# A fourth buffer of probabilities and three tiles of row maxima and exponents ahead, in the attention of the third layer

## The chip, the cores and the metric

The kernel is one program on one NeuronCore of a Trainium2 chip. Its metric is the device time of a whole call in microseconds (us), as the median of several executions; lower is better. A core has five engines that run their own instruction streams in program order and meet only at semaphores: TensorE (PE in the profile), VectorE (DVE), ScalarE (ACT), GpSimd (POOL) and SyncE (SP, which starts the loads).

## The reference, cut to what matters

Three layers work on 256 latent tokens and 256 context tokens of width 1024. The first mixes an mLSTM with window attention, the second mixes retention with a state space scan, the third is a multi-head latent attention; each is followed by a feed-forward part. In all of them the latent tokens end up as the output. What the change touches is the core of the third layer's attention:

```
q: 16 heads x 256 latent queries x 96        (64 plain + 32 rotated)
k: 16 heads x 512 keys (context + latent) x 96
v: 16 heads x 512 keys x 64
for each head:  p = softmax(q k^T / sqrt(96));  o = p v      # 256 x 512, then 256 x 64
out = concat(o) @ w_out
```

## The kernel before, in words

The attention works on 32 tiles, `a` = 0 to 31. A tile is one head with one half (128) of the queries against all 512 keys. Four successive tiles hold both halves of two heads (`head_of`), so the tiles go in groups of four. Each engine has its own loop over the tiles, written out by hand, and the order within an engine is fixed by it. Five steps make a tile, in this chain:

- **scores(a)**, PE, line 873: one product of 96 x 128 by 96 x 512 into one of four PSUM banks (0, 1, 6, 7 by `a % 4`); for a >= 4 it waits until the exponents of tile a - 4 have been taken from that bank. In the profile it is two MATMUL records a tile, under the names `bank` (tiles 0 and 1 of a group) and `cond_a` (tiles 2 and 3).
- **peaks(a)**, DVE, lines 2099 and 2100: the row maximum of the scores, and its product with the negative scale of the query. It waits for scores(a).
- **exps(a)**, ACT, line 1248: exponents of the scores into the buffer `prob[a % 3]`, with their row sum. It waits for peaks(a), and for the transposes of tile a - 3, which read the same buffer.
- **divide(a)**, DVE, lines 2108 and 2109: reciprocal of the row sum, and the buffer times it. It waits for exps(a).
- **turn(a)**, PE, line 881: four transposes of 128 x 128 into PSUM bank 2 (even a, name `bank`) or bank 3 (odd a, name `cond_b`). It waits for divide(a).
- **keep(a)**, ACT, line 1261: copies the four transposes to `turned`.

Once a group is through, **values(p)** on PE (line 893, 16 MATMUL records) multiplies the transposed probabilities of two heads with v, and **outputs(p)** on DVE (lines 1703 and 1706) splits the result into the high and the low part that the output projection reads.

The orders in which the engines issue this are what the change is about. PE starts with scores(0) to scores(3). Then for each a it issues turn(a), and only when a is odd, right behind it, scores(a + 3) and scores(a + 4); when a % 4 is 1 (and a > 4), values(a // 4 - 1) comes behind these. DVE starts with peaks(0) and peaks(1), and then for each a issues

```
divide(a)
if a + 2 < 2 * heads:
    peaks(a + 2)
if a >= 7 and (a - 7) % 4 == 0:
    outputs((a - 7) // 4)
```

ACT starts with exps(0) and exps(1), and then for each a issues keep(a) and exps(a + 2). The output projection (`linear("out2")`, lines 502 to 504) starts when the last outputs is done. No weights are rounded and hardly any are loaded while the attention runs: their slots are full. The buffer `work` (three rows of 512) holds squares ahead of the attention and again behind it, and is not used during it.

Of the kernel before, what the change touches and what calls it, by code (L numbers as in the profile page):

```python
# [8 lines left out]
ACT = mybir.ActivationFunctionType  # L9
# [4 lines left out]
P = 128  # L14
# [161 lines left out]
def build(nc, dram, small_at, tables_at, layers=3):  # L176
# [4 lines left out]
    with ExitStack() as stack:  # L181
        def sb(name, shape):
            return stack.enter_context(nc.sbuf_tensor(name, shape, F32))
# [5 lines left out]
        def sem(name):  # L189
            return stack.enter_context(nc.semaphore(name))  # L190
# [35 lines left out]
        work = sb("work", [P, 3, TOK])  # L226
# [27 lines left out]
        ident, ones, halves = (fixed[:, i * P:(i + 1) * P] for i in range(3))  # L254
# [17 lines left out]
        def limit(layer):  # L272
            return ARENA - max(b for _, b in tables_at[layer].values())


        c = Carve(arena, 0, limit(0))
# [11 lines left out]
                    turned=[c(4, LAT) for _ in range(4)], peak=c(32), nmax=c(32), total=c(32), esink=c(32), nsink=c(8))  # L288
# [4 lines left out]
        c = Carve(spare, 0, SPARE)  # L293
        narg = [c(2, 2, LAT) for _ in range(2)]
        junk_m = [junk_m] + [c(MD) for _ in range(2 * MH - 1)]
        c = Carve(arena, 0, limit(0))
        first_ada, cond_t, ada_rows = c(16, 1024), c(KD, 32), c(2, LAT)
        c = Carve(arena, 0, limit(1))
# [5 lines left out]
        c = Carve(spare, 0, SPARE)  # L304
# [5 lines left out]
        c = Carve(scratch, 0, 8192)  # L310
# [12 lines left out]

        c = Carve(arena, 0, limit(2))
        qh, kh, vl = c(LH, LAT), c(LH, TOK), c(TT, 1024)
        att2 = dict(prob=[c(512) for _ in range(3)], turned=[c(4, LAT) for _ in range(4)])
        c = Carve(spare, 0, SPARE)
        ckv, rope_s, kpe, kswap = c(2, TOK), c(4, LAT), c(TOK), c(LAT)
        rope_q = ckv.rearrange("p a (b t) -> p (a b) t", b=2)
# [29 lines left out]
        s = {n: sem(n) for n in names}  # L359
# [129 lines left out]
        def _(pe):  # L489
# [376 lines left out]
            def attention(m, a0, heads, q, k, v):  # L866
                count = 2 * heads

                def scores(a):
                    h, t = head_of(a)  # L870
                    if a >= 4:
                        pe.wait_ge(s["att_e"], a0 + a - 3)
                    pe.matmul(score_bank(a)[:, :], q(h)[:, t * P:(t + 1) * P], k(h),  # L873
                              start=True, stop=True).then_inc(s["att_s"], 1)

                def turn(a):
                    pe.wait_ge(s["att_p"], a0 + a + 1)
                    if a >= 2:
                        pe.wait_ge(s["att_pt"], a0 + a - 1)
                    for i in range(TT):  # L880
                        last = pe.transpose(bank[2 + a % 2][:, i * P:(i + 1) * P],  # L881
                                            m["prob"][a % 3][:, i * P:(i + 1) * P], ident)
                    last.then_inc(s["att_t"], 1)

                def values(p):

                    pe.wait_ge(s["att_pt"], a0 + 4 * p + 4)
                    if p >= 2:
                        pe.wait_ge(s["att_y"], a0 // 4 + p - 1)
                    for i in range(TT):  # L890
                        for e in range(2):
                            h = 2 * p + e
                            last = pe.matmul(bank[4 + p % 2][64 * e:64 * e + 64, 0:LAT], v(h, i),  # L893
                                             m["turned"][h % 4][:, i, :], start=(i == 0), stop=(i == TT - 1))
                    last.then_inc(s["att_o"], 1)

                for a in range(4):
                    scores(a)
                for a in range(count):
                    turn(a)  # L900
                    if a % 2:
                        for n in (a + 3, a + 4):
                            if n < count:
                                scores(n)
                    if a % 4 == 1 and a > 4:
                        values(a // 4 - 1)
                values(heads // 2 - 1)
# [256 lines left out]
        def _(act):  # L1164
# [76 lines left out]
            def attention(m, a0, heads, scale, sinks):  # L1241
                def exps(a):
                    h, t = head_of(a)
                    act.wait_ge(s["att_m"], a0 + a + 1)
                    if a >= 3:
                        act.wait_ge(s["att_t"], a0 + a - 2)
                    src = m["masked"][a % 3] if sinks else score_bank(a)[:, :]
                    e = act.activation(m["prob"][a % 3], src, ACT.Exp, bias=m["nmax"][:, a:a + 1],
                                       scale=scale if sinks else m["q_scale"][:, t:t + 1],
                                       accum_out=m["total"][:, a:a + 1])  # L1250
                    if sinks:
                        e = act.activation(m["esink"][:, a:a + 1], S("sink")[:, h:h + 1],
                                           ACT.Exp, bias=m["nmax"][:, a:a + 1])
                    e.then_inc(s["att_e"], 1)

                def keep(a):
                    h, t = head_of(a)
                    act.wait_ge(s["att_t"], a0 + a + 1)
                    if h >= 4:
                        act.wait_ge(s["att_o"], a0 // 4 + h // 2 - 1)  # L1260
                    act.activation(m["turned"][h % 4][:, :, t * P:(t + 1) * P],
                                   bank[2 + a % 2][:, :].rearrange("p (k q) -> p k q", k=TT),
                                   ACT.Copy).then_inc(s["att_pt"], 1)

                exps(0)
                exps(1)
                for a in range(2 * heads):
                    keep(a)
                    if a + 2 < 2 * heads:
                        exps(a + 2)  # L1270

            def out_and_squares(name, t0, t1):
                f = ph[name]
# [136 lines left out]
            for h in range(MH):  # L1410
# [6 lines left out]
                e = prob_m[h % 3]  # L1417
                for d in range(2):
                    for i in range(2):
                        act.activation(e[:, d * TT + i, :], bank[h % 2][:, d * LAT:(d + 1) * LAT], ACT.Exp, scale=-1.0,  # L1420
                                       bias=g_bias[:, d, i, h:h + 1])
                for d in range(2):
                    for i in range(2):
                        last = act.activation(e[:, d * TT + 2 + i, :], narg[h % 2][:, d, i, :], ACT.Exp,
                                              bias=g_bias[:, d, 2 + i, h:h + 1])
# [270 lines left out]
        def _(dve):  # L1696
# [386 lines left out]
            def attention(m, a0, heads, scale, sinks, tile0):  # L2083
                if sinks:
                    then(dve.tensor_scalar(m["nsink"], S("sink"), -1.0, None, ALU.mult))

                def peaks(a):
                    h, t = head_of(a)
                    dve.wait_ge(s["att_s"], a0 + a + 1)
                    if sinks:  # L2090
                        if a >= 3:
                            dve.wait_ge(s["att_e"], a0 + a - 2)
                        then(dve.tensor_tensor_reduce(m["masked"][a % 3], score_bank(a)[:, :],
                                                      C0("window", 2)[:, t, :], 1.0, -3e38, ALU.add, ALU.max,
                                                      m["peak"][:, a:a + 1]))
                        dve.tensor_scalar(m["nmax"][:, a:a + 1], m["peak"][:, a:a + 1], -scale,
                                          m["nsink"][:, h:h + 1], ALU.mult, ALU.min).then_inc(s["att_m"], 1)
                    else:
                        then(dve.reduce_max(m["peak"][:, a:a + 1], score_bank(a)[:, :], AX_X))
                        dve.tensor_scalar(m["nmax"][:, a:a + 1], m["peak"][:, a:a + 1], m["q_minus"][:, t:t + 1], None,  # L2100
                                          ALU.mult).then_inc(s["att_m"], 1)

                def divide(a):
                    dve.wait_ge(s["att_e"], a0 + a + 1)
                    one = m["total"][:, a:a + 1]
                    if sinks:
                        then(dve.tensor_tensor(one, one, m["esink"][:, a:a + 1], ALU.add))
                    then(dve.reciprocal(one, one))
                    dve.tensor_scalar(m["prob"][a % 3], m["prob"][a % 3], one, None, ALU.mult)\  # L2109
                       .then_inc(s["att_p"], 1)  # L2110

                def outputs(t):

                    dve.wait_ge(s["att_o"], a0 // 4 + t + 1)
                    y = bank[4 + t % 2][:, 0:LAT]
                    hi = h_hi[:, tile0 + t, L0:L1]
                    then(copy(hi, y))
                    low(h_lo[:, tile0 + t, L0:L1], y, hi).then_inc(s["att_y"], 1)

                peaks(0)  # L2120
                peaks(1)
                for a in range(2 * heads):
                    divide(a)
                    if a + 2 < 2 * heads:
                        peaks(a + 2)
                    if a >= 7 and (a - 7) % 4 == 0:
                        outputs((a - 7) // 4)
                outputs(heads // 2 - 1)
                dve.wait_ge(s["att_y"], a0 // 4 + heads // 2)
# [571 lines left out]
```

## Time and profile before

| | |
|---|---|
| median of 3 runs | 1650.05 us (1647.73 to 1653.05) |
| the profiled execution | 1653.18 us |
| its span, from the first to the last instruction | 1651.5 us |
| PE, DVE, ACT, POOL busy | 90%, 55%, 41%, 48% of the span |
| attention of the third layer, first scores to the first matmul of the output projection | 1349.16 to 1419.63 us |

"Busy" is the time in which an engine has an instruction running. The numbers in brackets of a timeline are idle time of the engine just before the instruction, and what released it. A granted clock of 1.00 is TensorE's full 2.4 GHz, 0.50 is 1.2 GHz. A MATMUL's end is modelled; its start is not, so starts are what one subtracts.

### The profile page before, as it was taken

To read this page: it belongs to the slowest core of one execution; us is meant where nothing else is said; L and a number is where in the kernel's file an instruction comes from. 1 tells how busy PE (TensorE), PEld (TensorE's weight loads), DVE (VectorE), ACT (ScalarE), POOL (GpSimd) and SP (SyncE) were. 2 spreads that over 40 slices of the span, in tenths; PEclk is the share of its full clock that TensorE was granted. 3 is DMA by queue.
4 is the path that set the end of the run, shared out by engine and by line. 5 is a ranking of instruction groups with operands and counts; after the bars stand their busy time and mean duration, and the time that the engine had idled before them with its cause. 6 is when DMAs were issued, how large, how long until landed. Compare 5 with 4: busy or idle time off the path is not lost.

```text
span 1651.5 us, 22264 instructions
## 1 busy us (share of the span) xinstructions
PE 1480.3 (90%) x8780; PEld 1237.0 (75%) x8780; DVE 910.2 (55%) x1569; ACT 672.6 (41%) x1076; POOL 784.6 (48%) x359
## 2 busy tenths in 40 slices
PE   5879877999995999887798999999998999899997
PEld 3767756999994887834377888888887874789997
DVE  3379956777674569455657644441015867444411
ACT  3325635544443123355344232232224566554442
POOL 0223504677781443364443444444443560468885
PEclk9789989999996999886798999999998999999999
DMA  9436603566672663200034555553332340345563
GB/s 368 181 128 242 227 30 141 189 232 231 225 246 89 213 220 104 67 11 26 1 125 143 179 193 188 182 197 95 91 99 70 112 131 1 92 146 185 189 180 117
DMA packets 71304, 242.97 MB, mean 147 GB/s; under 512 B 7456, under 2 KB 13088, under 8 KB 70816
## 3 DMA queue, kind: packets, MB, share of 16 engines
q1 hardware_dynamic: 68784, 237.15, 42.8%
q10 hardware_dynamic: 2416, 4.39, 0.9%
q8 instruction: 70, 1.15, 0.3%
q14 instruction: 34, 0.28, 0.1%
HBM read 239.42 MB, written 1.05 MB: 146 GB/s over the span
## 4 chain that ended last, share of the span: by engine, by line
PE 48%; DVE 5%; ACT 1%; issue 1%; POOL 0%; DVEq 0%; ACTq 0%
PE bank L502 14%; PE bank L504 14%; PE bank L503 14%; PE cond_a L933 1%; PE bank L873 1%; DVE arena L2501 1%; PE cond_b L951 1%; PE cond_b L881 0%; DVE h_lo L1706 0%; PE bank L893 0%; PE cond_b L893 0%; DVE arena L2109 0%; PE bank L960 0%; DVE scratch L2372 0%; PE bank L519 0%
## 5 line engine op out<-in xcount | busy, mean ns | idle before, releaser
L1649 POOL TENSOR_TENSOR w_lo<-raw,w_hi 128x1024 fp32r<-128x1024 f32 (+3 forms) x306 | 722.7, 2367 | 798.3 <-ACT w_hi L1179 797.7
L502 PE MATMUL bank<-h_hi,w_hi 128*128 128x256 f32 (+2 forms) x1664 | 558.3, 336 | 45.6 <-POOL w_lo L1649 18.6
L1179 ACT ACTIVATE w_hi<-raw 128x1024 fp32r<-128x1024 f32 (+3 forms) x306 | 314.5, 1030 | 644.0 <-PE bank L504 600.4
L503 PE MATMUL bank<-h_lo,w_hi 128*128 128x256 f32 (+2 forms) x1664 | 552.8, 332 | 0.0
L504 PE MATMUL bank<-h_hi,w_lo 128*128 128x256 f32 (+2 forms) x1664 | 552.3, 332 | 0.0
L502 PEld LDWEIGHTS bank<-h_hi,w_hi 128*128 128x128 f32 (+1 forms) x1664 | 318.3, 191 | 87.3 <-POOL w_lo L1649 31.9
L504 PEld LDWEIGHTS bank<-h_hi,w_lo 128*128 128x128 f32 (+1 forms) x1664 | 317.8, 191 | 32.6
L503 PEld LDWEIGHTS bank<-h_lo,w_hi 128*128 128x128 f32 (+1 forms) x1664 | 318.4, 191 | 31.5
L1706 DVE TENSOR_TENSOR hidden_lo<-work,hidden_hi 128x256 fp32r<-128x256 f32 (+1 forms) x66 | 111.0, 1681 | 160.3 <-ACT hidden_hi L1233 160.3
L502 PE MATMUL bank<-hidden_hi,w_hi 128*128 128x256 f32 (+1 forms) x528 | 168.9, 320 | 1.6 <-POOL w_lo L1649 1.6
L503 PE MATMUL bank<-hidden_lo,w_hi 128*128 128x256 f32 (+1 forms) x528 | 168.7, 320 | 0.0
L504 PE MATMUL bank<-hidden_hi,w_lo 128*128 128x256 f32 (+1 forms) x528 | 168.7, 320 | 0.0
L1724 DVE CUSTOM_DVE_ANT_0 ada_junk<-ada_w,cond_a 128x1024 bf16<-128x1024 f32 x128 | 153.6, 1214 | 20.9 <-DVE work L2193 7.7
L2179 DVE SCALAR_TENSOR_TENSOR X<-bank,mod,X 128x256 f32<-128x256 f32 x64 | 29.3, 481 | 207.7 <-PE bank L504 207.7
L502 PEld LDWEIGHTS bank<-hidden_hi,w_hi 128*128 128x128 f32 x528 | 99.6, 189 | 9.8 <-POOL w_lo L1649 1.8
L504 PEld LDWEIGHTS bank<-hidden_hi,w_lo 128*128 128x128 f32 x528 | 99.6, 189 | 7.9
L503 PEld LDWEIGHTS bank<-hidden_lo,w_hi 128*128 128x128 f32 x528 | 99.6, 189 | 7.9
L1703 DVE TENSOR_SCALAR arena<-bank 128x512 f32<-128x512 f32 (+2 forms) x64 | 37.9, 597 | 87.8 <-PE bank L504 87.2
L1724 DVE CUSTOM_DVE_ANT_0 ada_junk<-ada_w,cond_b 128x1024 bf16<-128x1024 f32 x64 | 77.8, 1216 | 0.0
L502 PE MATMUL bank<-w_hi,h_hi 128*128 128x256 f32 x160 | 50.2, 314 | 12.1 <-DVE arena L1703 5.8
L2193 DVE TENSOR_TENSOR work<-work,bank 128x256 f32<-128x256 f32 (+1 forms) x66 | 33.2, 503 | 44.2 <-PE bank L504 35.2
L1225 ACT ACTIVATE h_hi<-work,mod 128x256 fp32r<-128x256 f32 x80 | 36.4, 501 | 42.9 <-DVE work L1818 42.9
(378 smaller groups left out, 1810.7 us busy)
## 6 DMA issues: line engine op xcount, KB each, us to landing
raw<-in_up SPq DMA_DIRECT2D x132, 512.0 KB, 3.5
ada_w<-in_ada SPq DMA_DIRECT2D x128, 512.0 KB, 4.5
raw<-in_down SPq DMA_DIRECT2D x48, 448.0 KB, 3.5
raw<-in_out SPq DMA_DIRECT2D x24, 512.0 KB, 3.6
raw<-in_down SPq DMA_DIRECT2D x24, 512.0 KB, 3.5
raw<-in_in SPq DMA_DIRECT2D x24, 512.0 KB, 3.7
arena<-in_ada SPq DMA_DIRECT2D x16, 512.0 KB, 11.8
raw<-in_uq SPq DMA_DIRECT2D x12, 384.0 KB, 3.0
```

Source lines behind the costliest of these rows:

```text
L502: pe.matmul(out, w_h, x_h, start=first, stop=False)
L503: pe.matmul(out, w_h, x_l, start=False, stop=False)
L504: return pe.matmul(out, w_l, x_h, start=False, stop=last)
L873: pe.matmul(score_bank(a)[:, :], q(h)[:, t * P:(t + 1) * P], k(h), start=True, stop=True).then_inc(s["att_s"], 1)
L1179: act.activation(part_slot(w_hi, f, u), raw_slot(f, u), ACT.Copy).then_inc(s["rounded"], 1)
L1225: last = act.activation(h_hi[:, k, a:b], work[:, k % 3, a:b], ACT.Identity, bias=mod[:, n % 2, 24 * which + k, m:m + 1])
L1649: pool.tensor_tensor(part_slot(w_lo, f, u), raw_slot(f, u), part_slot(w_hi, f, u).bitcast(F32), ALU.subtract).then_inc(s["split"], 1)
L1703: return dve.tensor_scalar(out, in_, 1.0, None, ALU.mult)
L1706: return dve.tensor_tensor(out, x, hi.bitcast(F32), ALU.subtract)
L1724: dve.tensor_tensor_reduce(ada_junk[:, ada_sums[0] % 2, :], ada_w[:, k % SLOTS, :], silu_c[m][:, :], 1.0, 0.0, ALU.mult, ALU.add, mod[:, n ...
L2179: last = dve.scalar_tensor_tensor(out=X[:, k, a:e], in0=b[:, a - t0:e - t0], scalar=mod[:, layer[0] % 2, 8 * chunk + k, m:m + 1], in1=X[:, ...
L2193: dve.tensor_tensor(w, w, bank_of(f.first_taken + 2 * i + 1)[:, 0:t1 - t0], ALU.mult)\
```

## The change

A fourth buffer of probabilities is added, on the first row of `work`. The probabilities of tile a lie in `prob[a % 4]`, and exps(a) waits for the transposes of tile a - 4 in place of a - 3. DVE's loop begins with peaks(0) to peaks(2) and issues peaks(a + 3) behind divide(a), in place of peaks(a + 2). ACT's loop begins with exps(0) to exps(2) and issues exps(a + 3) behind keep(a), in place of exps(a + 2). PE's loop stays as it is but for the buffer that it reads: scores(a + 3) and scores(a + 4) are still issued behind turn(a) of an odd a.

```diff
-        att2 = dict(prob=[c(512) for _ in range(3)], turned=[c(4, LAT) for _ in range(4)])
+        att2 = dict(prob=[c(512) for _ in range(3)] + [work[:, 0, :]], turned=[c(4, LAT) for _ in range(4)])
...
-                                            m["prob"][a % 3][:, i * P:(i + 1) * P], ident)
+                                            m["prob"][a % 4][:, i * P:(i + 1) * P], ident)
...
                 def exps(a):
...
-                    if a >= 3:
-                        act.wait_ge(s["att_t"], a0 + a - 2)
+                    if a >= 4:
+                        act.wait_ge(s["att_t"], a0 + a - 3)
...
-                    e = act.activation(m["prob"][a % 3], src, ACT.Exp, bias=m["nmax"][:, a:a + 1],
+                    e = act.activation(m["prob"][a % 4], src, ACT.Exp, bias=m["nmax"][:, a:a + 1],
...
-                exps(0)
-                exps(1)
+                for a in range(3):
+                    exps(a)
                 for a in range(2 * heads):
                     keep(a)
-                    if a + 2 < 2 * heads:
-                        exps(a + 2)
+                    if a + 3 < 2 * heads:
+                        exps(a + 3)
...
-                    dve.tensor_scalar(m["prob"][a % 3], m["prob"][a % 3], one, None, ALU.mult)\
+                    dve.tensor_scalar(m["prob"][a % 4], m["prob"][a % 4], one, None, ALU.mult)\
...
-                peaks(0)
-                peaks(1)
+                for a in range(3):
+                    peaks(a)
                 for a in range(2 * heads):
                     divide(a)
-                    if a + 2 < 2 * heads:
-                        peaks(a + 2)
+                    if a + 3 < 2 * heads:
+                        peaks(a + 3)
```

## Rows read from the trace of the kernel before

**Rows 1.** The page: its first line, and the busy time of the engines.

```profile
span 1651.5 us, 22264 instructions
PE 1480.3 (90%) x8780; PEld 1237.0 (75%) x8780; DVE 910.2 (55%) x1569; ACT 672.6 (41%) x1076; POOL 784.6 (48%) x359
```

**Rows 2.** Windows: stretch, its length, each engine's busy us, granted clock, DMA share, GB/s.

```profile
1347.06:1349.16 2.10, 0.00 (x0) 0.03 (x1) 1.95 (x1) 2.05 (x4) 2.10 (x2) 1.00 0.32 98
1349.16:1355.00 5.84, 5.84 (x13) 2.65 (x14) 4.04 (x11) 2.08 (x5) 2.06 (x1) 0.71 0.52 173
1374.50:1382.95 8.45, 7.66 (x41) 4.06 (x41) 6.52 (x19) 5.32 (x12) 0.00 (x0) 1.00 0.00 0
1399.85:1408.30 8.45, 7.66 (x41) 4.05 (x41) 6.51 (x19) 5.32 (x12) 0.00 (x0) 1.00 0.01 2
```

**Rows 3.** Timeline of one group: start us, us, engine, line, operation [idle before <-releaser].

```profile
1377.88 0.15 DVE L2108 RECIPROCAL spare<-spare 128x1 f32<-128x1 f32 x1
1378.07 0.48 DVE L2109 TENSOR_SCALAR arena<-arena,spare 128x512 f32<-128x512 f32 x1
...
1378.47 0.68 DVE L2099 TENSOR_REDUCE spare<-cond_a 128x1 f32<-128x512 f32 x1
...
1378.61 0.66 PE L881 MATMUL cond_b<-fixed,arena 128*128 128x128 f32 x4 [0.78 <-DVE arena L2109]
...
1379.11 1.88 PE L873 MATMUL bank<-arena 96*128 96x512 f32 x4
...
1380.17 0.69 DVE L2099 TENSOR_REDUCE spare<-bank 128x1 f32<-128x512 f32 x1 [0.17 <-PE bank L873]
...
1380.92 1.95 PE L893 MATMUL cond_b<-arena 128*64 128x256 f32 x16
1381.03 0.15 DVE L2108 RECIPROCAL spare<-spare 128x1 f32<-128x1 f32 x1
...
1381.62 0.69 DVE L2099 TENSOR_REDUCE spare<-bank 128x1 f32<-128x512 f32 x1
...
1382.91 0.42 DVE L1703 TENSOR_SCALAR h_hi<-cond_b 128x256 fp32r<-128x256 f32 x1 [0.36 <-PE cond_b L893]
...
1383.29 0.60 PE L881 MATMUL cond_b<-fixed,arena 128*128 128x128 f32 x4
1383.37 0.42 DVE L1706 TENSOR_TENSOR h_lo<-cond_b,h_hi 128x256 fp32r<-128x256 f32 x1
...
1384.88 0.16 DVE L2108 RECIPROCAL spare<-spare 128x1 f32<-128x1 f32 x1 [1.08 <-ACT arena L1248]
```

**Rows 4.** Timeline of the attention's start, same columns.

```profile
1349.16 2.35 PE L873 MATMUL bank<-arena 96*128 96x512 f32 x4 [2.10 <-DVE arena L2501]
...
1351.31 3.22 PE L873 MATMUL cond_a<-arena 96*128 96x512 f32 x4
...
1353.26 0.69 DVE L2099 TENSOR_REDUCE spare<-cond_a 128x1 f32<-128x512 f32 x1 [0.17 <-PE cond_a L873]
...
1354.12 0.15 DVE L2108 RECIPROCAL spare<-spare 128x1 f32<-128x1 f32 x1
```

**Rows 5.** Timeline of its end: tile 29's reciprocal, and the output projection's first matmul.

```profile
1411.67 0.15 DVE L2108 RECIPROCAL spare<-spare 128x1 f32<-128x1 f32 x1
...
1419.63 0.39 PE L502 MATMUL bank<-h_hi,w_hi 128*128 128x256 f32 x1 [0.98 <-DVE h_lo L1706]
```

**Rows 6.** Waits from 1370 to 1405 us: who, for whom, us in total, times, longest.

```profile
DVE spare L2108 <- ACT arena L1248: 4.3, 4, 1.1
```

**Rows 7.** PE's timeline around the end of the first layer's mLSTM.

```profile
255.03 0.66 PE L835 MATMUL cond_b<-fixed,arena 128*128 128x128 f32 x4 [1.76 <-DVE arena L2065]
255.52 0.60 PE L835 MATMUL bank<-fixed,arena 128*128 128x128 f32 x4
257.31 0.39 PE L502 MATMUL bank<-h_hi,w_hi 128*128 128x256 f32 x1 [1.18 <-DVE h_lo L1706]
```

**Rows 8.** The window around these gaps, columns as in rows 2.

```profile
251.00:261.00 10.00, 6.84 (x51) 5.83 (x50) 4.89 (x13) 8.32 (x14) 0.00 (x0) 1.00 0.00 0
```

## The prediction

> **What bounds the kernel now.** I read the page first: TensorE is busy for 1480.3 of 1651.5 us [rows 1], so over the whole call it is the bound, and no other engine comes above 55%. What the change touches is one stretch of some 70 us, and what that stretch is worth has to be read there. So next came the windows of the attention, one group of four tiles at a time. A group takes 8.45 us, the first full one and the last alike, and in it TensorE is busy for 7.66 us, VectorE for 6.52 and ScalarE for 5.32 [rows 2]. No engine is full: the stretch is bound by a ring of waits that runs through three engines. The timeline of one group shows the ring. VectorE waits 1.08 us for an exponent behind outputs [rows 3], and this comes once in every group: 4 waits of together 4.3 us in four groups [rows 6]. It waits 0.36 us for values and 0.17 us for scores; TensorE waits 0.78 us for a divided tile [rows 3]. The change goes at the 1.08: with three tiles ahead, that exponent would be long done. The reader should look for the opposite figure in the same rows, the 0.17 us: it says how little room is left between scores and row maxima.
>
> **The change part by part.** No instruction is added or removed: 32 of each kind stay, at the same shapes. The fourth buffer is ordinary on-chip memory of the same form, and `work` has no other user in the stretch; I put its cost at nothing, since a divide of 0.48 us [rows 3] does the same work at another address. If it did cost, the nearest row gives the bound: eight tiles use it, and one more divide for each would be 8 x 0.48 = 3.8 us; one saved would be as much to the other side. What changes is the order on VectorE and ScalarE. ScalarE has 8.45 - 5.32 = 3.13 us free per group [rows 2], and its earlier exponents can't block it for long, for what they wait for (row maxima) is what VectorE now issues first. Its part is nothing, and the loosened wait on the transposes too: exps(a + 3) stands behind keep(a), which has already waited for the transposes of tile a, one more than it needs.
>
> The order on VectorE is what decides. TensorE issues scores(a + 3) only behind turn(a), for odd a. Before, VectorE asks for these scores after divide(a), peaks(a + 2) and divide(a + 1); those last two are its cover, 1381.03 less 1380.17 or 0.86 us for the row maximum and 1381.62 less 1381.03 or 0.59 us for the divide, together 1.45 us, and it still comes 0.17 us too early [rows 3]. After the change, peaks(a + 3) comes right behind divide(a). The cover is gone, and VectorE stands still from the end of its divide until turn(a) and scores(a + 3) have run, once in every two tiles. What is queued behind the wait is the next divide, and for that waits the next turn on TensorE.
>
> The ring of the new order, from one odd tile's divide to the next odd tile's, with each step from start to start [rows 3]:
> - divide to turn: 1377.88 to 1378.61, 0.73
> - turn to scores: to 1379.11, 0.50
> - scores to row maximum: to 1380.17, 1.06
> - row maximum to the even tile's divide: to 1381.03, 0.86
> - this divide to the next row maximum: to 1381.62, 0.59 (its scores, right behind the others on TensorE, are ready by then: half of four records, 0.86 us later than the first)
> - this row maximum to the next odd divide: 0.86 again
>
> Together 4.60 us for two tiles. Where outputs stands in between, it is 0.92 more (two steps of 1382.91 to 1383.37, 0.46), so 5.52. Its values have long run by then, so it does not wait. Where values stands in between, TensorE is about as slow as this ring: turn to the last turn behind values is 1378.61 to 1383.29, 4.68 [rows 3], and I take that.
>
> The number of each: from the divide of tile 1 to that of tile 29 there are 14 such halves, 6 with outputs (behind tiles 7, 11, 15, 19, 23, 27), 6 with values (behind 5, 9, 13, 17, 21, 25), 2 plain. 6 x 5.52 + 6 x 4.68 + 2 x 4.60 = 70.4 us. A group in the steady part takes 5.52 + 4.68 = 10.2 us in place of 8.45.
>
> The start: divide(0) now comes behind a third row maximum, which begins at 1353.26 and is through at 1354.12 [rows 4]; then a divide of 0.59 and peaks(3) of 0.86, so divide(1) begins at 1355.57, and divide(29) at 1355.57 + 70.4 = 1425.97. Before, it begins at 1411.67 [rows 5]. Behind tile 29 no row maximum is left, so the end is the same chain as before, 1419.63 less 1411.67 or 7.96 us. The difference is 14.3 us, all of it on the path, since the output projection waits for the last outputs, as it does now.
>
> The clock is the part that the trace doesn't settle. In the half with outputs, TensorE now stands idle twice: from the end of the scores until the even turn (the divide comes 0.92 late, so its start is 0.73 + 0.50 + 1.06 + 0.86 + 0.92 + 0.73 = 4.80 us after the odd divide, the scores have ended at 0.73 + 0.50 + 1.72 = 2.95, which makes 1.85), and then 0.98 until the odd turn, with one turn in between. Before, the granted clock stays at 1.00 through every full group [rows 2]. Two rows stand on either side of the new case. An idle stretch of 2.10 us ahead of the attention [rows 4] is followed by a mean clock of 0.71 over 5.84 us, which means that part of it ran at 1.2 in place of 2.4 GHz and 0.29 x 5.84 = 1.7 us of full-speed work went missing [rows 2]. Gaps of 1.76 and 1.18 us with two turns between them, after the first layer's mLSTM, leave it at 1.00 throughout [rows 7, 8]. The new gaps lie between these. From none to six falls, one in each half with outputs, the price is 0 to 10.2 us. I take two, 3.4 us, as the new pair is nearer to the second row but has less work in between.
>
> The Trainium skill, page "TensorE: Matmul & The Clock Gate", section "A second HAM failure mode: psum-queue depth-cycling", says that where TensorE idles briefly and often between groups of matmuls, while it goes through accumulation banks in turn, its clock keeps moving between the two levels, and each move is paid again. The present kernel has such gaps in every group and no fall, so the trace does not bear the rule out at 0.78 us; by the rule the sum would be that of the second rival below.
>
> The sum: 14.3 + 3.4 = 17.7 us. The profiled execution would go from 1653.18 to 1670.9, its span from 1651.5 to 1669.2. The median of the runs lies 3.1 us below the profiled execution, and I take the same difference for the kernel after: 1650.05 + 17.7, or about 1668.
>
> **The rivals.**
> First, the wait for exponents is what the ring costs and nothing takes its place. Then TensorE would be the bound, and each of eight groups would lose the idle 8.45 - 7.66 = 0.79 us: 6.3 us faster, 1643.7. For it speaks that the 1.08 us wait is in every group. It needs scores(a + 3) to be there when VectorE gets to peaks(a + 3), 0.59 us after it began the odd divide; I count 0.73 + 0.50 + 1.06 = 2.29 us, so 1.70 us are missing. Since even the present order is 0.17 short, I give it 0.03.
> Second, the same ring, and the clock falls in each half with outputs, or in more: 14.3 + 10.2 = 24.5, or 1674.6. For it: the 2.10 us of idle time that was enough once. Against it: the pair of rows 7. 0.17.
> Third, no change: the new waits, two of 1.70 in a group, only take the place of the old ones. The old ones on VectorE come to 1.08 + 0.36 + 0.17 = 1.6 us in a group [rows 3], against 3.4 of the new, so each new wait would have to be half as long as the steps say. (The difference, 1.8 us, is that of 10.2 and 8.45 again, found the other way.) 1650, 0.04.
> Fourth, the ring holds in part: VectorE runs on into the next group while TensorE is late anyway, and the loss is about half of 14.3, 1657. The steps leave no room for it that I can see; 0.08.
>
> **How the numbers follow.** My forecast, the ring with none to four falls of the clock, has 0.68, and gives 1664.3 to 1671.1; with the errors of the steps, 1662 to 1672. The range of 8 in 10 takes in most of the second rival, and a part of the fourth: 1660 to 1677. A measurement of this kernel can tell about 0.3%, 5 us, from no change. Slower by more than that are the forecast, the second and the fourth: 0.93. Within it 0.04, faster 0.03.
>
> **What would show it.** In the changed kernel's timeline, TENSOR_REDUCE of L2099 on the bank of an even tile should be preceded by idle time of about 1.6 us released by L873, 14 times, on `bank` and `cond_a` in turn; the wait of 1.08 us at L2108 and that of 0.36 us at L1703 should be gone. A group should take 10.2 us at full clock. TensorE should wait some 1.8 us ahead of one turn in each group. A granted clock below 1.00 inside the attention, behind its first 6 us, shows the falls, each some 1.7 us. Outside the stretch from 1349 to 1434 nothing should move but in time. It would be wrong if the row maximum's wait is under 0.9 us, or if the group stays at 8.45 us or below.

## The result and the profile after

The changed kernel takes 1672.38 us in the median of 4 runs (1670.97 to 1673.12), beside 1648.89 for the kernel before in the same comparison: a ratio of 1.0146, 95% interval 1.0129 to 1.0163. It is 24 us (21 to 27) slower. The forecast was 17.7 us slower, and 1668 us with a range of 1660 to 1677.

TensorE's busy time in the page hardly grew, from 1480.3 us [rows 1] to 1491.5:

```profile
span 1670.1 us, 22263 instructions
PE 1491.5 (89%) x8780; PEld 1238.4 (74%) x8780; DVE 906.6 (54%) x1569; ACT 674.6 (40%) x1076; POOL 784.5 (47%) x359
```

The loss is in the attention. It runs from 1339.93 to 1438.66 us, 98.7 us, where it was 1349.16 to 1419.63, 70.5 us [rows 4, 5]. That it begins 9 us earlier is not the change: up to there both programs are the same, and over the profiled executions of all kernels below the attention began anywhere between 1339.9 and 1349.2 us (two of the changed kernel itself at 1339.93 and 1345.74). The two spans alone, 1651.5 and 1670.1, therefore mislead by up to that much; the length of the stretch is what one compares.

A half is the stretch from one odd turn to the next, two tiles long. In an outputs half VectorE also has outputs to do, in a values half TensorE also has values; a plain half has neither. The windows of the kernel after (columns as in rows 2): the start, all the rest, the two plain halves, a group in which the clock stayed up nearly to its end, and a group in which it did not.

```profile
1339.93:1345.93 6.00, 5.61 (x10) 2.24 (x11) 3.58 (x9) 3.35 (x7) 2.06 (x1) 0.72 0.51 169
1345.93:1438.66 92.73, 73.52 (x313) 37.26 (x311) 48.49 (x136) 42.88 (x92) 1.96 (x1) 0.82 0.00 1
1347.12:1356.29 9.17, 6.06 (x25) 2.98 (x25) 5.66 (x16) 5.66 (x13) 0.00 (x0) 1.00 0.00 1
1356.29:1366.28 9.99, 7.82 (x41) 4.07 (x41) 6.41 (x18) 5.36 (x13) 0.00 (x0) 0.95 0.00 0
1379.03:1392.23 13.20, 10.86 (x41) 5.36 (x41) 6.51 (x18) 5.54 (x13) 0.00 (x0) 0.75 0.00 1
```

Set beside the groups of before, 8.45 us at a clock of 1.00 [rows 2], these show two separate losses. A group at full clock takes 10.0 us in place of 8.45, and a group with a fallen clock 13.2. The busy time of VectorE in a group is 6.4 to 6.5 us as before, so nothing on it got slower; TensorE's rises from 7.8 to 10.9 with the same instructions, which is the lower clock.

The timeline of the first of these groups, with two halves from odd turn to odd turn (1356.29, 1360.96, 1366.28):

```profile
1355.56 0.15 DVE L2108 RECIPROCAL spare<-spare 128x1 f32<-128x1 f32 x1
...
1356.29 0.66 PE L881 MATMUL cond_b<-fixed,arena 128*128 128x128 f32 x4 [0.79 <-DVE arena L2109]
...
1356.78 1.88 PE L873 MATMUL bank<-arena 96*128 96x512 f32 x4
...
1357.84 0.69 DVE L2099 TENSOR_REDUCE spare<-bank 128x1 f32<-128x512 f32 x1 [1.61 <-PE bank L873]
...
1358.70 0.15 DVE L2108 RECIPROCAL spare<-spare 128x1 f32<-128x1 f32 x1
...
1359.29 0.68 DVE L2099 TENSOR_REDUCE spare<-bank 128x1 f32<-128x512 f32 x1
...
1360.96 0.60 PE L881 MATMUL cond_b<-fixed,work 128*128 128x128 f32 x4
...
1361.40 1.88 PE L873 MATMUL cond_a<-arena 96*128 96x512 f32 x4
...
1362.46 0.69 DVE L2099 TENSOR_REDUCE spare<-cond_a 128x1 f32<-128x512 f32 x1 [1.65 <-PE cond_a L873]
...
1363.32 0.41 DVE L1703 TENSOR_SCALAR h_hi<-cond_b 128x256 fp32r<-128x256 f32 x1
...
1364.11 0.15 DVE L2108 RECIPROCAL spare<-spare 128x1 f32<-128x1 f32 x1
...
1364.84 0.83 PE L881 MATMUL bank<-fixed,arena 128*128 128x128 f32 x4 [1.56 <-DVE arena L2109]
...
1366.28 1.12 PE L881 MATMUL cond_b<-fixed,arena 128*128 128x128 f32 x4 [0.61 <-DVE arena L2109]
```

The reader is to see three things. VectorE's row maximum, which waited 0.17 us [rows 3], now waits 1.61 and 1.65 us for scores, and right ahead of it stands the odd divide that TensorE's turn and scores are waiting for. The old waits are gone: no idle time ahead of outputs (1363.32) and none ahead of the reciprocal behind it (1364.11). And TensorE stands idle for 1.56 and then 0.61 us (0.78 in four of the five later groups, 0.53 in the other) around the turn of 1364.84. The turn of 1364.84 takes 0.83 us and that of 1366.28 takes 1.12, both in place of 0.66: the clock fell behind the stretch of 1.56 us, before the second came.

Who VectorE waits for, over the attention of the kernel after (us in total, times, longest):

```profile
DVE spare L2099 <- PE bank L873: 19.9, 13, 2.9
DVE spare L2099 <- PE cond_a L873: 18.5, 8, 3.3
DVE h_hi L1703 <- PE cond_b L893: 2.9, 1, 2.9
DVE h_hi L1703 <- PE bank L893: 2.8, 1, 2.8
```

No wait for an exponent is left of those that came once a group [rows 6]; in their place stand 38 us of waits for scores, 14 of them of 1.6 us or more. The longest of these, 3.3 us, are twice as long as the order alone makes them: TensorE at the lower clock comes to its scores late.

The same stretch where the clock is low, one values half (odd turn at 1379.03 to odd turn at 1386.91, 7.88 us in place of 4.67):

```profile
1379.03 1.11 PE L881 MATMUL cond_b<-fixed,arena 128*128 128x128 f32 x4 [0.78 <-DVE arena L2109]
...
1379.94 3.62 PE L873 MATMUL bank<-arena 96*128 96x512 f32 x4
...
1381.89 0.69 DVE L2099 TENSOR_REDUCE spare<-bank 128x1 f32<-128x512 f32 x1 [2.91 <-PE bank L873]
...
1383.49 3.00 PE L893 MATMUL cond_b<-arena 128*64 128x256 f32 x16
...
1386.91 0.60 PE L881 MATMUL cond_b<-fixed,work 128*128 128x128 f32 x4
```

Scores take 3.62 us in place of 1.88 and values 3.00 in place of 1.95, directly behind the pair of idle stretches. The fall lands on the half in which TensorE has the most to do and no slack.

All six outputs halves of this execution are followed by such a fall. Five stretch the values half behind them; the sixth stretches the last one, where no scores are left:

```profile
1429.80 0.93 PE L881 MATMUL cond_b<-fixed,arena 128*128 128x128 f32 x4 [0.78 <-DVE arena L2109]
...
1430.66 3.31 PE L893 MATMUL cond_b<-arena 128*64 128x256 f32 x16
...
1434.39 0.60 PE L881 MATMUL cond_b<-fixed,work 128*128 128x128 f32 x4
```

From turn to turn that is 4.59 us, where the kernel before takes 2.96.

### The profile page after: what moved, and what is told of

Read it like the earlier page. It is cut to its first block, busy times and chain, and to the rows that moved or that the text cites. A ratio compares the mean times of both kernels' runs of the same rounds, so it can differ in the third digit from the quotient of the medians.

```text
span 1670.1 us, 22263 instructions
## 1 busy us (share of the span) xinstructions
PE 1491.5 (89%) x8780; PEld 1238.4 (74%) x8780; DVE 906.6 (54%) x1569; ACT 674.6 (40%) x1076; POOL 784.5 (47%) x359
## 4 chain that ended last, share of the span: by engine, by line
PE 48%; DVE 6%; ACT 1%; issue 1%; POOL 0%; DVEq 0%; ACTq 0%
PE bank L502 14%; PE bank L503 14%; PE bank L504 14%; PE bank L873 1%; PE cond_a L933 1%; DVE spare L2099 1%; DVE arena L2501 1%; PE cond_b L881 1%; PE cond_b L893 1%; DVE h_lo L1706 1%; PE bank L893 1%; PE cond_b L951 1%; DVE arena L2109 1%; PE cond_a L873 0%; PE bank L519 0%
```

## The experiments

The theory: (1) VectorE asks for scores(a + 3) before TensorE has issued them, which costs some 13 us by itself; (2) the idle stretches that this leaves on TensorE lower its clock, which costs the rest. The rivals: the fourth buffer, ScalarE's new order, or three tiles ahead as such. Ratios are to the kernel before on the same chip, with 95% intervals; "length" is that of the attention in the profiled execution, from the first scores to the output projection (70.5 us before).

**The fourth buffer alone.** The two changes of order are undone, the buffer and its indices stay.

```diff
-                for a in range(3):
-                    exps(a)
+                exps(0)
+                exps(1)
...
-                    if a + 3 < 2 * heads:
-                        exps(a + 3)
+                    if a + 2 < 2 * heads:
+                        exps(a + 2)
...
-                for a in range(3):
-                    peaks(a)
+                peaks(0)
+                peaks(1)
...
-                    if a + 3 < 2 * heads:
-                        peaks(a + 3)
+                    if a + 2 < 2 * heads:
+                        peaks(a + 2)
```

> The fourth buffer alone, both orders as before. Theory: the exponent's wait for the transposes of three tiles back was long over, so no change: ratio 1.000 within 0.2%, group 8.45 us. Rival (a buffer in another place costs): up to 4 us slower, divides on it longer than 0.49 us.

Ratio 1.0012 (0.9999 to 1.0025), length 70.5 us, every full group 8.45 us. Divides in either place take the same time:

```profile
L2109 DVE TENSOR_SCALAR arena<-arena,spare x24: 485/486/489, 1348.8 to 1409.5; 128x512 f32<-128x512 f32 x24
L2109 DVE TENSOR_SCALAR work<-work,spare x8: 485/486/490, 1354.2 to 1410.9; 128x512 f32<-128x512 f32 x8
```

(duration in ns, least/median/most). The buffer costs and brings nothing.

**VectorE three ahead, ScalarE two.** As the changed kernel, with ScalarE's loop as before.

```diff
-                for a in range(3):
-                    exps(a)
+                exps(0)
+                exps(1)
...
-                    if a + 3 < 2 * heads:
-                        exps(a + 3)
+                    if a + 2 < 2 * heads:
+                        exps(a + 2)
```

> Four buffers, VectorE's row maxima three tiles ahead, ScalarE's exponents two ahead as before. Theory (VectorE asks for scores that TensorE has not issued; ScalarE's order plays no part): the same as the changed kernel, a ratio of 1.012 to 1.016, 14 waits for scores of 1.6 us or more, the clock falling too. Rival (ScalarE's order, exponents ahead of keeps, does the harm): as the kernel before, within 0.3%.

Ratio 1.0146 (1.0127 to 1.0165), length 92.3 us. VectorE's order alone does the whole harm of the change.

**ScalarE three ahead, VectorE two.** The other half of the change: as the changed kernel, with VectorE's loop as before.

```diff
-                for a in range(3):
-                    peaks(a)
+                peaks(0)
+                peaks(1)
...
-                    if a + 3 < 2 * heads:
-                        peaks(a + 3)
+                    if a + 2 < 2 * heads:
+                        peaks(a + 2)
```

> Four buffers, ScalarE's exponents three tiles ahead, VectorE's row maxima two ahead as before. Theory: the exponent of the next group's first tile no longer stands behind the keep that waits for values, so VectorE's wait of 1.08 us shrinks and nothing takes its place; worked out with the steps of the rows of before, a group goes from 8.45 to 7.7 us and the attention loses 4 us, ratio 0.997 to 0.998. Rival (ScalarE's order does the harm): slower by 5 us or more. Rival (that wait costs nothing, TensorE is the bound): no change.

Ratio 0.998 (0.9964 to 0.9995), length 65.9 us: 4.6 us shorter. From odd turn to odd turn it takes 3.09 and 4.68 us in turn, 7.77 a group. VectorE's waits there: short ones for scores and values, and the wait for an exponent only once in place of once a group:

```profile
DVE spare L2099 <- PE bank L873: 2.8, 9, 1.3
DVE spare L2099 <- PE cond_a L873: 2.7, 8, 0.4
DVE h_hi L1703 <- PE cond_b L893: 1.3, 4, 0.4
...
DVE spare L2108 <- ACT work L1248: 0.3, 1, 0.3
```

So the wait that one would have aimed at was worth something, and this half of the change takes it away.

**TensorE kept at work in the gaps.** The changed kernel, with products that nobody reads, written to the bank that the turn then overwrites. (The edit also puts the turn's wait for the divided tile behind its other wait, for every tile. In the plain halves, ahead of any extra product, the idle stretch ahead of the even turn is 0.86 us with it, in place of 0.77.)

```diff
                 def turn(a):
-                    pe.wait_ge(s["att_p"], a0 + a + 1)
                     if a >= 2:
                         pe.wait_ge(s["att_pt"], a0 + a - 1)
+                    if a >= 8 and a % 4 < 2:
+                        for n in (512, 256) if a % 4 == 0 else (256,):
+                            pe.matmul(bank[2 + a % 2][:, 0:n], q(0)[:, 0:P], k(0)[:, 0:n],
+                                      start=True, stop=True)
+                    pe.wait_ge(s["att_p"], a0 + a + 1)
```

> The changed kernel, with TensorE kept at work in the two gaps of each half with outputs: from tile 8 on, one extra product of 512 columns and one of 256 ahead of the turn of the first tile of a group, one of 256 ahead of that of the second, written to the turn's own bank and overwritten by it. Theory (order of the waits costs 14 us less 1.2 for the shorter outputs, the falling clock the rest): granted clock 1.00 in the attention behind its first 6 us, a group of 5.3 + 4.7 = 10.0 us, the attention 13 us longer than before (83.5 us from the first scores to the output projection), the call 13 us or 1.008 over the kernel before. Rival (the fourth buffer or the order slows the values halves themselves, clock or not): values halves stay at 6.4 to 7.9 us and the call at 1.014. Rival (extra matmuls delay the turns): above 1.014.

Ratio 1.0099 (1.0081 to 1.0118), length 85.1 us. With more work on TensorE, 1.45 and 0.60 us of it in each group, the kernel is faster than the changed one. Its windows behind the first 6 us, and from the values of the first group to the end:

```profile
1352.14:1431.20 79.06, 69.81 (x348) 37.71 (x345) 48.07 (x136) 42.83 (x91) 1.96 (x1) 0.98 0.00 1
1366.00:1431.20 65.20, 59.77 (x313) 32.70 (x312) 40.83 (x116) 35.23 (x75) 1.96 (x1) 1.00 0.00 1
```

One fall came ahead of the extra products, in the second plain half (5.95 us in place of 4.59, 1.36 more); from there on the clock is at 1.00, and all values halves take 4.65 to 4.68 us and all outputs halves 5.34 or 5.35. Without that fall the length would be 83.7 us, 13.2 above before: this is the price of the order at full clock. The call's 16 us (13 to 19) agrees with the 14.6 us of the length.

**Less of it.** One product of 512 columns ahead of the first turn of a group, none ahead of the second; the cut is shown against the last experiment.

```diff
-                    if a >= 8 and a % 4 < 2:
-                        for n in (512, 256) if a % 4 == 0 else (256,):
-                            pe.matmul(bank[2 + a % 2][:, 0:n], q(0)[:, 0:P], k(0)[:, 0:n],
-                                      start=True, stop=True)
+                    if a >= 8 and a % 4 == 0:
+                        pe.matmul(bank[2 + a % 2][:, :], q(0)[:, 0:P], k(0), start=True, stop=True)
```

> The changed kernel with less extra work for TensorE: one product of 512 columns (0.86 us) ahead of the turn of each group's first tile from tile 8 on, and none ahead of the second's, so that idle stretches of about 1 us on either side of that turn are left. Theory (a pair of idle stretches of 1 us does not lower the clock, as a pair of 0.8 us does not in the kernel before): no fall behind the start, attention 83.7 to 85 us, ratio 1.009. Rival (what counts is idle time summed over the pair, and 2 us of it is enough): two or more falls, attention of 88 us or more, ratio 1.011 to 1.015.

Ratio 1.0112 (1.0082 to 1.0142), length 88.7 us. Here the theory missed, and the figures are its rival's: behind the fall in the plain half there are two more (values halves of 6.29 and 6.31 us in place of 4.65). The first of the two:

```profile
1373.46 0.66 PE L883 MATMUL bank<-fixed,arena 128*128 128x128 f32 x4 [0.70 <-DVE arena L2111]
...
1374.99 0.63 PE L883 MATMUL cond_b<-fixed,arena 128*128 128x128 f32 x4 [0.88 <-DVE arena L2111]
1375.46 3.15 PE L873 MATMUL bank<-arena 96*128 96x512 f32 x4
```

So idle stretches of 0.70 and 0.88 us are enough now and then: the same pair stands in all six groups and the clock fell behind two of them. The rival's rule, that the sum of the two decides and 2 us are enough, is not shown by this; the sum here is 1.58 us. Nor does the kernel before have a pair, as the expectation has it: it has one stretch of 0.78 us a group.

**The changed kernel once more.**

> The changed kernel once more, to see how much of its attention is the clock's doing and how far that moves from one execution to the next. Theory: ratio 1.013 to 1.016; plain halves 4.6 us, outputs halves 5.3 us as in the first profile, and only the values halves differ, with a length that follows the low stretches. Rival (the lengths are set by waits alone): every half as long as in the first profile.

Ratio 1.0157 (1.0137 to 1.0177), length 92.3 us against 98.7 in the first profile. The windows behind the first 6 us, of this execution:

```profile
1351.74:1438.04 86.30, 66.89 (x313) 34.84 (x310) 48.26 (x136) 42.82 (x91) 1.97 (x1) 0.88 0.00 1
```

The mean clock is 0.88 where the first had 0.82. Plain halves take 4.58 and 4.59, outputs halves 5.32 in both. Of the values halves three are stretched here (7.62, 6.33, 7.39 us), and five in the first (6.37 to 7.88); the last one is stretched in both, to 4.45 and 4.59 us in place of 2.96. That makes four falls here and six in the first. In the kernel with VectorE alone three ahead it is four.

**Scores behind every turn.** The changed kernel, with TensorE's order made to fit it.

```diff
                 for a in range(count):
                     turn(a)
-                    if a % 2:
-                        for n in (a + 3, a + 4):
-                            if n < count:
-                                scores(n)
+                    if a + 4 < count:
+                        scores(a + 4)
```

> The changed kernel, with TensorE issuing scores(a + 4) behind every turn(a), in place of two behind every second turn. Theory (the harm lies in the distance between the row maxima and the scores in TensorE's order): the distance is now the same for every tile, one turn and one divide of cover; by the steps of the rows of before a group takes 8.7 us in place of 10.2, and with fewer idle stretches the clock falls less; the call is 2 to 8 us slower than before, ratio 1.001 to 1.005. Rival (three tiles ahead is harmful in itself, through ScalarE or the buffers): stays at 1.014.

Ratio 1.0018 (1.0006 to 1.003), length 74.5 us; halves of 4.02 and 4.68, 8.70 a group. With both of VectorE's and ScalarE's changes left as they are, 24 us shrink to 3. Most of the harm is the distance between two orders. Not all of it is gone: once a group VectorE still waits 1.79 us, for scores that TensorE issues behind values, and TensorE then stands idle for 1.12 us ahead of a turn. That alone never lowered the clock here. At the very end, where a second stretch follows, it fell, and values took 3.63 us in place of 1.95:

```profile
1406.90 0.66 PE L881 MATMUL bank<-fixed,arena 128*128 128x128 f32 x4 [1.12 <-DVE arena L2107]
...
1408.35 0.66 PE L881 MATMUL cond_b<-fixed,arena 128*128 128x128 f32 x4 [0.79 <-DVE arena L2107]
...
1408.93 3.63 PE L893 MATMUL cond_b<-arena 128*64 128x256 f32 x16
```

**The same in the kernel before**, with two tiles ahead and three buffers.

> The kernel before, with TensorE issuing scores(a + 4) behind every turn(a). Theory: the 0.17 us wait for scores and a part of TensorE's wait for the divide go; by the same steps a group takes 7.5 us in place of 8.45, the attention is 6 us shorter, ratio 0.996 to 0.997. Rival (the wait of 1.08 us for the exponent behind outputs sets the group's length): no change.

Ratio 0.9971 (0.9957 to 0.9986), length 65.0 us, 7.59 a group (2.91 and 4.68). VectorE's waits there; the one for the exponent stays (0.9 us, eight times), those for scores are left at the start:

```profile
DVE spare L2106 <- ACT arena L1246: 7.1, 8, 0.9
...
DVE spare L2097 <- PE bank L873: 1.6, 2, 1.3
```

**Both that help.** Scores behind every turn, ScalarE three ahead, VectorE two ahead.

> Scores behind every turn, four buffers, exponents three ahead on ScalarE, row maxima two ahead on VectorE: both changes that should each help. Theory: by the steps, a group takes 7.2 to 7.3 us, which is TensorE's own work, so that the two gains do not add in full: 7 to 8 us shorter than before, ratio 0.995 to 0.996. Rival (each gains on its own): 10 us, 0.994. Rival (neither wait was on the ring): no change.

Ratio 0.9948 (0.993 to 0.9966), 1639.55 us, length 61.5 us: 9.0 us less than before and the fastest order of all. One group of it:

```profile
1359.97:1367.19 7.22, 7.22 (x41) 4.06 (x40) 6.38 (x19) 5.42 (x12) 0.00 (x0) 1.00 0.01 2
```

TensorE is busy for 7.22 of 7.22 us. The two gains, 4.6 and 5.4 us of length, come close to adding up (9.0 of 10.0). That they stop there because only TensorE's own work is left is an estimate: four scores of 0.86 us, values of 1.88 (1380.92 to the turn at 1382.80 in the kernel before) and four turns of 0.44 to 0.50 (from a turn to the scores behind it) make 7.1 to 7.3 us. The busy time alone would not show it, since matmul ends are modelled.

This kernel differs from the one of "Scores behind every turn" only in that VectorE looks two tiles ahead and not three, and it is 13.1 us shorter (61.5 and 74.5; 1.7 us of this is the fall at the end of the latter). With TensorE's old order the same step cost 17.8 us at full clock (65.9 and 83.7). So VectorE's third tile ahead costs time with either order of TensorE's.

**The same with three buffers.** As the last, with `prob[a % 3]` and without the fourth buffer.

> Scores behind every turn, exponents three ahead on ScalarE, row maxima two ahead, and three buffers of probabilities as before. Theory (exps(a + 3) stands behind keep(a), which has waited for the transposes of the same buffer, so a fourth buffer has nothing to do): as with four buffers, 61.5 us of attention, ratio 0.993 to 0.997. Rival (the fourth buffer is what lets the exponents run ahead): back towards 65 us and 0.997 or above.

Ratio 0.9928 (0.9907 to 0.9949), 1637.34 us, length 61.5 us. The fourth buffer is not needed for it: exps(a + 3) is issued behind keep(a), which has waited for the transposes that last read the buffer. Both versions beat the kernel before and the changed one; their intervals overlap.

## Why the prediction was right, and where it was off

- **What bounds the attention: a ring of waits.** Right. Changes of order alone, with no instruction added, gave groups of 7.22 to 10.0 us.
- **The buffer costs nothing.** Right: 1.0012, and 486 ns for a divide on either memory.
- **ScalarE's part is nothing.** For the changed kernel right (1.0146 without it). Alone it is not nothing but a gain of 4.6 us, hidden in the change by VectorE's new wait.
- **The new wait for scores, 1.6 us, once in two tiles.** Right: 14 times, 1.61 and 1.65 us at full clock. This settles the third rival, which needed waits half as long, and the 13.2 us at full clock settle the fourth, which had half of 14.3. TensorE's new idle time was put at 1.85 and 0.98 us and is 1.56 and 0.78.
- **The ring, 4.60, 4.68 and 5.52 us a half.** Measured 4.59, 4.67 and 5.32. The last is 0.20 too long: outputs costs 0.79 and not 0.92 before the next reciprocal starts (1363.32 to 1364.11), and the scores start 0.44 and not 0.50 behind the turn (1360.96 to 1361.40). Six halves of 0.20 are 1.2 us, so 14.3 should have been 13.1; the extra products show 13.2.
- **The clock, 3.4 us.** This is the term that was mis-sized. The sum took two falls at 1.7 us; the profiles of the changed kernel have six and four, which make 15.0 and 8.6 us (98.7 and 92.3 less 83.7), or 2.5 and 2.2 us each. From the runs it is 24 less 13.2, about 11 us (8 to 14). Two things were wrong in it. The step put the new gaps between two rows, 2.10 us that led to a fall and 1.76 with 1.18 us that did not [rows 4, 7], and leaned to the second; but a single case without a fall says little of a pattern that comes back in every group. And 1.7 us for each is what one fall costs at the attention's start; here a stretched half with scores is 1.7 to 3.2 us longer, since the clock stays down for longer (the group from 1379.03 at 0.75 loses 0.25 x 13.2 = 3.3 us of full-speed work) and nearly all of it falls on the half where TensorE has no slack. The second rival, at 0.17, named what happened, a fall behind every outputs half in one profile and behind four of six in the other. That its sum, 24.5 us, is so close to the 24 measured is in part luck: its ring was 1.2 us too long and its falls too cheap, at 1.7 us each where 2.2 to 2.5 were measured. The rule of the Trainium skill that stood beside it ("TensorE: Matmul & The Clock Gate", "A second HAM failure mode: psum-queue depth-cycling", on idling between groups of matmuls) was the better guide: the trace of before did not bear it out at 0.78 us, that of after does at 1.56 and 0.78.
- **The total.** The forecast of 1668 us lies 4 us below the measured time, and its 17.7 us lie 6 below the 24; the kernel before came out 1.2 us lower in the second comparison, which hides a part. The ring was 1.2 us too long and the clock some 8 us too cheap, so the range held because it had been made wide enough for most of the second rival.
- **The faster rival.** It fell for the reason given, missing cover: the scores are not there when VectorE asks for them. That cover is worth time was seen in the kernel before as well: with scores one turn earlier for half of the tiles it gains 5.4 us.

What stays open: why the number of falls differs from one execution to the next (0.82 and 0.88 of full clock for the same program), and how small a pair of idle stretches must be to be safe. One stretch a group, of 0.78 us in the kernel before or 1.12 with scores behind every turn, never led to a fall. Of pairs, 0.77 and 0.79 in the plain halves of the changed kernel did not, 0.70 and 0.88 did behind two groups of six, and 1.56 and 0.78 behind six of six in one profile and four of six in another.

## What to carry to other kernels

A deeper look-ahead on a consumer that works in program order can only wait earlier, with its other work queued behind the wait, unless the producer's order runs as far ahead. Count, for each new position, how many instructions stand between the producer's issue and the consumer's request, and on which engine the producer is itself waiting. Here one more tile ahead on VectorE overtook TensorE's scores. Moving the scores by one turn gained 5.4 us, the fourth buffer nothing, and with the scores moved two tiles ahead on VectorE were still better than three (61.5 and 74.5 us). And price new idle time on TensorE twice: once as the wait, here 13.2 us, and again as the clock that may fall behind it, here about 11.

## What the runs showed of the hardware

- Added matmuls made a kernel faster: with 1.45 and 0.60 us of unread products in each group, the attention went from 92.3 to 98.7 us down to 85.1, since the granted clock stayed at 1.00 from the first of them on.
- A fall of the clock moves what it costs to the instructions behind it: the idle time was in the outputs halves, which kept their 5.32 us, and the values halves behind them went from 4.67 us to as much as 7.88.
- TensorE's clock also fell once in a stretch with idle times of 0.86 and 0.81 us ahead of two turns in a row, in the plain halves of the two kernels with extra products, ahead of the first of these. In the same halves of the changed kernel the stretches are 0.77 and 0.79 us, and it did not fall.
